# Whole-model kernel on one core: MLPs written out with a split norm, expert weights in another row order, w_mod products spread over more stages

## What is computed

```python
def first_block(x, ...):
    for i in range(DEPTH):
        h = rmsnorm(x, norm_mix[i])
        y = gated_deltanet_bidir(h, ...) if i == 0 else dilated_window_attention(h, ...)
        x = x + y
        h = rmsnorm(x, norm_mlp[i])
        x = x + squared_relu_mlp(h, mlp_w1[i], mlp_w2[i])      # 1024 -> 4096 -> 1024
    return rmsnorm(x, norm_final)

def second_block(x, c, ...):
    c_act = jax.nn.silu(c)
    for l in range(DEPTH):
        mod = (c_act @ w_mod[l] + b_mod[l])[:, None, :]         # w_mod[l]: 1024 x 6144
        sh1, sc1, g1, sh2, sc2, g2 = jnp.split(mod, 6, axis=-1)
        h = rmsnorm_2(x, norm1_g[l]) * (1.0 + sc1) + sh1
        proj = h @ w_in[l]
        ...
        x = x + g1 * (merged @ w_out[l])
        h2 = rmsnorm_2(x, norm2_g[l]) * (1.0 + sc2) + sh2
        x = x + g2 * ec_moe(h2, w_router[l], w_gate[l], w_up[l], w_down[l])
    return rmsnorm_2(x, final_g)
```

## Time and profile before

| | before |
|---|---|
| median of 3 runs | 2812.88 us (2812.69 to 2819.08) |
| the profiled execution | 2815.55 us |
| its span | 2813.5 us |
| PE busy | 2197.7 us (78%) |
| DVE (VectorE) busy | 802.9 us (29%) |
| ACT (ScalarE) busy | 509.2 us (18%) |
| read from HBM | 639.62 MB |
| mean granted TensorE clock | 0.859 |

### The profile page before, as it was taken

The page is one execution under the profiler, slowest core; times in us unless marked ns, Lnnn a source line. Parts: engine busy times, 40 slices in busy tenths (PEclk is TensorE's granted clock), DMA queues, the critical chain, the costliest instruction groups (busy, mean ns, idle before and its releaser), DMA issues.

```text
span 2813.5 us, 34009 instructions
## 1 busy us (share of the span) xinstructions
PE 2197.7 (78%) x13912; PEld 1432.0 (51%) x13912; DVE 802.9 (29%) x1562; ACT 509.2 (18%) x944; POOL 30.5 (1%) x49
## 2 busy tenths in 40 slices
PE   7866658998997997979976666665989977666665
PEld 6655546777674776748742222222748742222221
DVE  4534443892023796121130000002121130000001
ACT  3221123441132442031010000001021010000000
POOL 0010000000000000000000000000000000000000
PEclk9977769999958998989978888877979978778887
DMA  7310005855026795323329999999323319999997
GB/s 281 110 71 2 2 1 178 318 221 210 8 87 257 256 336 195 122 90 120 150 83 403 401 401 403 403 401 389 135 90 120 137 62 403 403 401 401 403 403 274
DMA packets 242850, 642.03 MB, mean 228 GB/s; under 512 B 9471, under 2 KB 19013, under 8 KB 242373
## 3 DMA queue, kind: packets, MB, share of 16 engines
q1 hardware_dynamic: 242757, 640.72, 60.4%
HBM read 639.62 MB, written 1.09 MB: 228 GB/s over the span
## 4 chain that ended last, share of the span: by engine, by line
PE 45%; SPq 31%; DVE 12%; issue 5%; DVEq 3%; DMA 2%; ACT 2%; POOL 1%; ACTq 0%; POOLq 0%
SPq L360 30%; PE psum L1038 6%; DVE arena L1422 4%; PE psum L725 4%; PE psum L936 3%; PE psum L925 2%; PE psum L850 2%; PE psum L549 2%; DVEq L1421 2%; PE psum L1052 2%; DMA ring<-in_w_down 2%; DVE arena_r L1199 1%; PE psum L751 1%; PE psum L752 1%; PE psum L753 1%
## 5 line engine op out<-in xcount | busy, mean ns | idle before, releaser
L1113 PE MATMUL psum<-ring,arena 128*32 128x256 f32 x4096 | 304.1, 449 | 201.4 <-DMA ring<-in_w_up 161.3
L1113 PEld LDWEIGHTS psum<-ring,arena 128*32 128x32 f32 x4096 | 144.2, 125 | 363.8 <-issue 168.1
L1133 PE MATMUL psum<-ring,arena 128*32 128x512 f32 x1024 | 180.9, 843 | 112.3 <-DMA ring<-in_w_down 108.0
L1741 DVE TENSOR_TENSOR arena<-psum,arena 128x256 f32<-128x256 f32 x32 | 13.6, 424 | 589.2 <-PE psum L1113 589.2
L1038 PE MATMUL psum<-h_featmajor,ring 128*128 128x256 f32 x768 | 173.8, 379 | 1.6 <-DVE arena L1660 1.6
L1038 PEld LDWEIGHTS psum<-h_featmajor,ring 128*128 128x128 f32 x768 | 145.8, 190 | 22.2 <-DVE arena L1660 2.5
L1199 DVE TENSOR_TENSOR arena_r<-ring,arena_r 128x2048 fp32r<-128x2048 f32 x64 | 143.0, 2287 | 42.5 <-ACT arena_r L1787 41.6
L1133 PEld LDWEIGHTS psum<-ring,arena 128*32 128x32 f32 x1024 | 35.2, 136 | 220.4 <-DMA ring<-in_w_down 115.0
L2053 ACT ACT_TABLE_LOAD x32 | 41.1, 1283 | 556.1 <-PE psum L1113 556.1
L1787 ACT CAST arena_r<-ring 128x2048 fp32r<-128x2048 f32 x64 | 119.8, 1904 | 80.1 <-PE psum L753 80.1
L1745 DVE COPY arena<-psum 128x512 f32<-128x512 f32 x64 | 44.3, 692 | 304.4 <-PE psum L1133 304.4
(11 more groups left out here) (358 smaller groups left out, 2908.0 us busy)
## 6 DMA issues: line engine op xcount, KB each, us to landing
ring<-in_w_gate SPq DMA_DIRECT2D x64, 2048.0 KB, 19.1
ring<-in_w_up SPq DMA_DIRECT2D x64, 2048.0 KB, 21.9
ring<-in_w_down SPq DMA_DIRECT2D x64, 2048.0 KB, 24.4
ring<-in_mlp_w SPq DMA_DIRECT2D x32, 2048.0 KB, 8.8
ring<-in_w_mod SPq DMA_DIRECT2D x24, 2048.0 KB, 8.1
ring<-in_w_in SPq DMA_DIRECT2D x20, 2048.0 KB, 10.3
ring<-in_gdn_w_in SPq DMA_DIRECT2D x8, 2048.0 KB, 19.5
ring<-in_dswa_w_in SPq DMA_DIRECT2D x6, 2048.0 KB, 19.3
```

What stands on the lines that cost most here:

```text
L1113: ins = mm(PS[32 * j:32 * j + 32, 4 + m, 0:T], XGE[:, 4 * u + kk, :], W(v + 2 * m + u, D)[:, kk, j * T:(j + 1) * T], start=u == 0 and kk = ...
L1133: ins = mm(PS[32 * j:32 * j + 32, yb, :], HTE[:, cc, 32 * j:32 * j + 32], W(v + 4 + u, 512)[:, 2 * j + cc, :], start=cc == 0, stop=cc == 1 ...
```

## The change

1. *Row order.* `pmajor(w)` reads w as "(p k) n -> p k n": partition p gets the eight rows 8p to 8p + 7. w_gate and w_up are read so (four whole rows of 4096 bytes that lie behind each other, so 16,384 bytes), as are w_in_2 and w_router_2; w_down comes with `halves`. The features of the second block's h stand in the same order: the transposes of the norm read every eighth column (`by_rows`), the parameters b_mod_2, norm1_g_2 and norm2_g_2 are loaded in it (PMC), and the gate row GR is written so. w_down's product makes both column halves with each unit.
2. *MLPs.* The loop is written out. The low part of a weight is written over the weight in its ring slot, and the slot is released by PE when it has used it. `norm_split` works by tile of tokens: ScalarE writes the high part straight from PSUM, VectorE the low part, and PE begins units 0 and 1 with tile 0 alone.
3. *w_mod.* MLP 0 has units 0 to 5 (one in each of six hidden units), the DSWA projections units 6 to 17, MLP 1 units 18 to 23. The sum over partitions is eight products with a column of ones (`mod_cols`, L582 of the changed kernel), in the place of transposes and reductions.

```diff
-U_MLP = (11, 49)
+U_MLP = (11, 55)
-U_SIN, U_SOUT = 39, 46
+U_SIN, U_SOUT = 33, 52
+def dswa_unit(u):
+    return U_SIN + (0, 2, 5, 8, 11, 14, 18)[u]
+MOD_UNITS = ([U_MLP[0] + 5 + 3 * j for j in range(6)] + [U_SIN + 1] + [U_SIN + 3 * u + i for u in range(1, 6) for i in range(2)]
+             + [U_SIN + 17] + [U_MLP[1] + 5 + 3 * j for j in range(6)])
@@ SP @@
+            def mod(g):
+                load(MOD_UNITS[g], cols(A["w_mod_2"][g // 12], 512 * (g % 12), 512 * (g % 12 + 1)))
             for u in range(7):
-                load(U_SIN + u, cols(w, 512 * u, min(512 * (u + 1), 3456)))
+                load(dswa_unit(u), cols(w, 512 * u, min(512 * (u + 1), 3456)))
+                if u == 0:
+                    mod(6)
+                elif u < 6:
+                    mod(2 * u + 5)
+                    mod(2 * u + 6)
+                if u == 5:
+                    mod(17)
+            def pmajor(w):
+                return w.rearrange("(p k) n -> p k n", p=P)
                     for m, name in enumerate(("w_gate_2", "w_up_2")):
                         for u in range(2):
-                            load(U_SEC + V_MOE + 2 * m + u, halves(two(A[name]), u), tu + e)
+                            load(U_SEC + V_MOE + 2 * m + u, pmajor(two(A[name]))[:, 4 * u:4 * u + 4, :], tu + e)
                     for u in range(2):
-                        load(U_SEC + V_MOE + 4 + u, cols(two(A["w_down_2"]), 512 * u, 512 * (u + 1)), tu + e)
+                        load(U_SEC + V_MOE + 4 + u, halves(two(A["w_down_2"]), u), tu + e)
@@ PE @@
+            def mod_cols(m):
+                for g in (2 * m, 2 * m + 1):
+                    spent(pe, MOD_UNITS[g])
+                if m >= 1:
+                    pe.wait_ge(sem("mod_out"), m)
+                for k in range(KC):
+                    ins = mm(PS[:, 6, k:k + 1], MA[m % 2].rearrange("p (q k) -> p k q", k=KC)[:, k], ones[:, 0:1], start=True, stop=True)
+                ins.then_inc(sem("mod_mm"), 1)
+                norm_split(k_norm, 0)
+                up(0, 0, 0)
+                up(1, 0, 1)
+                norm_split(k_norm, 1)
+                up(0, 1, 4)
+                up(1, 1, 5)
+                turn(0)
+                pe.wait_ge(sem("act_lo"), NU * l + 1)
+                down(0, True, False)
+                for u in range(1, NU - 1):
+                    up(u + 1, 0, 4)
+                    turn(u)
+                    up(u + 1, 1, 5)
+                    pe.wait_ge(sem("act_lo"), NU * l + u + 1)
+                    down(u, False, False, {3: 9 * l, 5: 9 * l + 1}.get(u))
+                turn(NU - 1)
+                pe.wait_ge(sem("act_lo"), NU * l + NU)
+                mod_cols(9 * l + 2)
+                down(NU - 1, False, True)
@@ PE, DSWA chunks @@
+                if ch in (4, 7, 10, 13, 16):
+                    mod_cols(2 + ch // 3)
+            pe.wait_ge(sem("mod_out"), 8)
@@ VectorE @@
+            def split_rest(s, t, scale):
+                for dc in range(KC):
+                    if dc % 4 == 0:
+                        dve.wait_ge(sem("h_hi"), 16 * s + 8 * t + dc + 4)
+                    ts = slice(t * P, (t + 1) * P)
+                    v.scalar_tensor_tensor(HT_R[:, dc, ts], PS[:, 4 + 2 * t + dc // 4, (dc % 4) * P:(dc % 4 + 1) * P], scale(dc),
+                                           HTH_R[:, dc, ts].bitcast(F32), ALU.mult, ALU.subtract).then_inc(sem("ht_ready"), 1)
+                for u in range(NU):
+                    if u < NU - 1:
+                        low(l, down_unit(u))
+                    hidden_low(u)
+                    if u < NU - 2:
+                        low(l, up_unit(u + 2))
+                    elif u == NU - 2:
+                        low(l, down_unit(NU - 1))
+                    if 1 <= u < NU - 1:
+                        mod_unit(18 * l + u - 1)
+                    if u in (3, 5, 7):
+                        mod_sum(9 * l + (u - 3) // 2)
@@ VectorE, DSWA projections @@
+            for m in range(3, 9):
+                if m == 8:
+                    mod_sum(7)
+                mod_unit(2 * m)
+                mod_unit(2 * m + 1)
+                if 4 <= m < 8:
+                    mod_sum(m - 1)
@@ ScalarE @@
+            def norm_split(r, s, x_count, scale):
+                mean_square(r, x_count)
+                act.wait_ge(sem("rstd_ready"), r * 2 + 1)
+                a.activation(XN[:, 0, :], X[:, 0, :], ACT.Copy, scale=rstd[:, 0:1]).then_inc(sem("xn0"), 1)
+                for t in range(TT):
+                    act.wait_ge(sem("ht_psum"), 3 * s + t + 2)
+                    for dc in range(KC):
+                        a.activation(HTH_R[:, dc, t * P:(t + 1) * P], PS[:, 4 + 2 * t + dc // 4, (dc % 4) * P:(dc % 4 + 1) * P],
+                                     ACT.Copy, scale=scale(dc)).then_inc(sem("h_hi"), 1)
```

More of the change, by code:

```diff
@@ L156, in both @@
             return plain, sb(name + "_r", shape, F32R)
-        ring = sb("ring", [P, RING, SLOT])
+        slots = [both(f"ring{i}", [P, SLOT]) for i in range(RING)]
+        ring, ring_r = [s[0] for s in slots], [s[1] for s in slots]
         X = sb("x_resid", [P, TT, D])
@@ L237, in program @@
         c = Carve(0)
-        RL = c(TT, 512)
+        HALF = SLOT // 2
+        WH = [ar_r[:, x * HALF:(x + 1) * HALF] for x in range(4)]
+        HTH_R = ar_r[:, 4 * HALF:5 * HALF].rearrange("p (a b) -> p a b", b=T)
+        c.at = 14336
+        RL = [c(TT, 512), c(TT, 512)]
+        MT_R = ar_r[:, c.at:c.at + 1024].rearrange("p (a b) -> p a b", b=T)
         MT = c(4, T)
-        MT_R = ar_r[:, 1024:2048].rearrange("p (a b) -> p a b", b=T)
+        MTH_R = ar_r[:, c.at:c.at + 1024].rearrange("p (a b) -> p a b", b=T)
         c(4, T)
[L242 to L252, removed]
+        MA = [c(1024), c(1024)]
+        c.at = 10240
+        FGR = c(1024)
         c = Carve(0)
@@ L406, in mlp @@
             def mlp(l):
[L407 to L423, removed]
+                w1, w2 = A["mlp_w1"][l], A["mlp_w2"][l]
+                load(mlp_unit(l, up_unit(0)), cols(w1, 0, 512))
+                for u in range(NU):
+                    if u + 1 < NU:
+                        load(mlp_unit(l, up_unit(u + 1)), cols(w1, 512 * (u + 1), 512 * (u + 2)))
+                    load(mlp_unit(l, down_unit(u)), halves(w2, u))
+                    if 1 <= u < NU - 1:
+                        mod(18 * l + u - 1)
             mlp(0)
@@ L770, in up, with down @@
                         ins.then_inc(sem("up_mm"), 1)
-                def down(idx, n, turns, count, hf, first, last):
-                    halves_ = ((hf, idx + hf),) if not last else ((0, idx), (1, idx + 1))
-                    split = {f: parts("w2", i, n, turns, count) for f, i in halves_}
+                    else:
+                        used(ins, mlp_unit(l, i))
+                def down(u, first, last, m=None):
+                    i = down_unit(u)
                     if last:
-                        order = [(b, 2 * f + kk) for b in range(4) for f in range(2) for kk in range(2)]
-                    else:
-                        order = [(b, 2 * hf + kk) for kk in range(2) for b in range(4)]
+                        halves_ = [parts(i, 0), parts(i, 1)]
+                        order = [(b, k) for b in range(4) for k in range(4)]
+                    else:
+                        halves_ = [parts(i, 0), None]
+                        order = [(b, k) for k in range(4) for b in range(4)]
                     for b, k in order:
                         t, h = b // 2, b % 2
-                        wh, wl = split[k // 2]
+                        if halves_[k // 2] is None:
+                            halves_[1] = parts(i, 1)
+                        wh, wl = halves_[k // 2]
                         c = slice((k % 2) * D + h * 512, (k % 2) * D + (h + 1) * 512)
```

415 lines of the change are left out of this document (197 added, 218 removed).

## The result

| | before | after |
|---|---|---|
| median | 2812.78 us (4 runs, 2808.73 to 2819.08) | 2840.82 us (4 runs, 2835.66 to 2849.19) |
| the profiled execution | 2815.55 us, span 2813.5 | 2837.28 us, span 2835.1 |
| PE busy | 2197.7 us | 2220.1 us |
| DVE busy | 802.9 us | 789.0 us |
| mean granted TensorE clock | 0.859 | 0.864 |

A forecast was written before the change was run, and what follows sets the result against it. Expert loops were taken as bound by bytes and row length, MLPs by TensorE and VectorE. Expert rows -45, MLPs -17, DSWA +56, small parts -1 gave -7, so 2806 us; its own range 2790 to 2822, full range 2782 to 2837.

The forecast's parts named there:

- Expert rows, -45: Both expert loops: w_gate and w_up in 16 KB rows, w_down in 4 KB rows, save 22.5 us per loop.
- long rows gain nothing: Rival, expert loops: w_gate and w_up gain nothing from longer rows, 27 us lost, total 2833 us; chance 0.17.
- MLPs, -17: Both MLPs: TensorE alone sets iterations, 23.1 us instead of 25.2, plus earlier starts; -8.8 and -8.1 us.
- early starts: MLP starts: split norm lets first products begin after half a tile, at 445.5 against 453.2, and 895.1 against 900.5.
- new wait: MLPs, after the transposes of hidden unit 0: PE waits before the first down product, 5.5 us with clock loss.
- eight one-column products, 0.15 each, 1.2 us a time: w_mod column sums, three times per MLP and in DSWA: 1.2 us per group, bounds 0.6 and 2.2.
- DSWA, +56: DSWA projections: w_mod loads, products and ring slots make PE stop, so the stage ends near 160 us instead of 104.
- upper bound of +66: DSWA projections: the term's upper bound, with column groups of 2.2 us and a little more wait per stop.
- only follows its bytes: Rival, DSWA: stops and slots cost little, last products at about 120 us, +16, total 2766 us; chance 0.08.
- Strided reads, up to +18: Rival, second block's transposes: reading every eighth column costs some 200 loads 0.19 us again, total up to 2824; chance 0.10.
- third rival: MLPs keep their 25 us through ScalarE casts and splits waiting for PE's slots; total about 2817 us; chance 0.10.
- first rival: The rival "long rows gain nothing", expert loops: slower if w_gate and w_up stay under about 413 GB/s; 2833 us; chance 0.17.

The follow-up runs named there:

- experiment 3: Changed kernel, with VectorE accumulating w_mod sums in natural order and only the last multiply-add writing strided, so TensorE reads contiguous columns: 2821.22 us (1.0043 of before).
- experiment 5: Changed kernel with TensorE making the column sums one stop later in the DSWA projections: 2802.17 us (0.9972 of before).
- contig_last2: The run of experiment 3: changed kernel, only VectorE's last multiply-add per w_mod unit writes strided, weight reads contiguous: 2821.22 us.
- Experiment 1: Changed kernel with only the first of eight one-column products made in each of the twelve groups (modulation values wrong): 2796.93 us (0.9945 of before).
- best3b: best2 with w_down in rows of 8192 bytes, TensorE turning every second column of the hidden tile: 2751.92 us (0.9797 of before).
- best2: Changed kernel with later DSWA stops, one strided write per w_mod unit, and each MLP's last group ahead of the hidden-tile wait: 2768.00 us (0.9870 of before).

## Why the prediction was wrong

*Expert rows, -45: right*, in size (-45.3) and cause: a linear price per row, read from two lengths, carried to 8 and 16 KB. The rival "long rows gain nothing" named the right side of the result for the wrong reason: the kernel is slower, but not by this place.

*MLPs, -17: wrong, +4.8 seen.* The early starts, the new wait and the 23.2 us iteration came as written. The step that failed, here and in DSWA, is "eight one-column products, 0.15 each, 1.2 us a time". The row it rested on the earlier trace rows counts 32 records for 16 products, 0.22 us a product; I took 0.15 below it, with no row for that, and the upper bound of 2.2 left out the stride, though the text named strided reads a few lines on and gave them 0 "as for any weight load". Measured: 3.73. Three per MLP make 3 x 2.6 = 7.8 us each. Part of the 2.6 is the count (a contiguous group takes 1.84 and not 1.2), the larger part the stride. The forecast also had no loss of clock around a group: the iterations with one should take 26.9 us and took 26.9 and 28.1 in MLP 0, 29.4 and 28.4 in MLP 1, where the granted clock was 0.89 in the first of them (1066 to 1096); with contiguous groups (experiment 3) all four took 25.0, which is 23.2 and the group. And the start of tile 0 was slow in MLP 1 (13.9 us for what took 11.3 in MLP 0). What the iterations were to gain, 13 us per MLP, came but for 2: from the first to the last transposes of the hidden tile MLP 0 took 168.7 us before and 165.1 now, of which two groups are 7.5.

*DSWA, +56: the mechanism right, the size short by 18.* The forecast had stops of 13 and 16 us at chunks 13 and 16, for the slots of units 2 and 3: 12.8 and 16.5 seen. The error is again the columns: 6 x (3.93 - 1.2) = 16.4. Of these six some ran at the lower clock behind a stop, where contiguous groups took 3.54 too; the forecast had 2 us for the clock after a stop, and kept the group at 1.2. The upper bound of +66 took 2.2 for a group and so missed too. The rival "only follows its bytes" (about 120 us for the stage) falls with the 176.6 seen, and experiment 5 shows the stops' place as the cause.

*Together*: the twelve groups make 15.6 + 16.4 = 32 us, against an error of 29 in the profiled executions (-7 forecast, +22 seen). The MLPs (6) and DSWA (2) lost 8 beyond the groups, and what was not in the sum, or priced at nothing, came to about -11 (table). That these nearly cancel is luck. The largest of them, layer 1's 8.3 us, can't be put down to the change: in contig_last2 the same instructions took 7.5 us longer than in the changed kernel, at a granted clock of 0.88 against 0.91 over the stage. Experiment 1 shows the groups from the other side: with them nearly gone the kernel lands where it was forecast, with the same luck in it.

*Strided reads, up to +18:* this rival came true, where the moving side is one column: without the stride the kernel took 20 us less (experiment 3). Its size was luck, for 200 loads of 0.19 us are 38 and not 18. The norm's transposes, of which the text spoke, cost nearly nothing: the 16 before layer 0 went from 3.43 to 3.68 us, layer 0's projections and attention from 342.1 to 343.2.

*Other slips on record*, none of which moved the forecast: the bounds added in quadrature are 31 us upwards and 12 downwards, not 16; of 2790 to 2822 a bit under half lies below 2804.5; with MLP iterations at 25 us in both MLPs the third rival comes to some 2827 and not 2817; and the first rival's limit for w_gate's rate is near 418 GB/s and not 413.

## What to carry to other kernels

Count a small matmul in records and weight loads, not in products: with one moving column its price followed the weight load (0.115 us a record for loads of 0.192, 0.233 for loads of 0.335), and the load's price its stride. When an engine must stop for work that comes through a ring of buffers, put the stop behind the instructions that free the buffer it waits for; here three chunks later was worth 38 us with the same loads. And price a load by its rows: here 75 ns per 2 KB and 10 ns a row told the loops with 8 and 16 KB from the rates at 2 and 4 within 0.5%.

## What the runs showed of the hardware

- Weight load of 128 columns fp32, medians: 0.192 us contiguous, 0.197 with stride 2, 0.335 with stride 8. A turned hidden tile in best3b paid more for stride 2 (shortest load 0.193 us, 0.138 in best2).
- Engine at 1.2 GHz after a stop of 13 us: sixteen records in 3.54 us contiguous and 3.93 strided; at 2.4 GHz 1.84 and 3.73.
- Around a group of strided column sums of 3.73 us the granted clock was below 1.00 though PE never idled: 0.93 and 0.89 in two windows above, but 1.00 in 538 to 565. In contig_last2, with groups of 1.84 us, all four such windows showed 1.00. What decides it was not tried.
- VectorE's multiply-add of 128x512 fp32 with strided operands: 1.115 us instead of 0.751.
- HBM loads by rows of 2, 4, 8 and 16 KB: 387 and 410 GB/s, and loops of 467, 458 and 453 us, one core running; 428 while only rows of 16 KB landed. 422 in the plateaus, against the 358 that the Trainium skill ("DMA: Bandwidth & Descriptors", Where 436 GB/s comes from) gives as what binds loads from HBM; the measurement decides.
